# A differential attention stage with a new order of work on every engine

## The chip, the cores and the metric

The kernel runs on one core of a Trainium2 chip. A core has five engines that run their own instruction lists and meet only at semaphores: PE (TensorE, matmuls into the eight PSUM banks), DVE (VectorE), ACT (ScalarE), POOL (GpSimd) and SP (SyncE, which here only issues DMAs). The metric is the device time of one execution in microseconds (us).

## The reference

Two post-norm residual layers over 512 positions of width 1024, in float32. Layer 0 mixes tokens by a chunked spatial gate, layer 1 by differential attention; behind each mixer comes a gated feed-forward block with a width-3 convolution. The change lies in the attention alone:

```python
q, k, v = split(x @ w_qkv)            # 8 heads; q and k as 2 halves of 64, v 128 wide
logits  = q_half @ k_half.T / 8 + bias[head]
probs   = softmax(logits)             # 2 maps of 512 x 512 per head
attn    = probs[0] - lam * probs[1]
o       = attn @ v                    # 512 x 128 per head
o       = o * rsqrt(mean(o * o) + eps) * subln_g * (1 - lambda_init)
y       = concat(o) @ w_out
```

## The kernel before, in words

**Numbers in two halves.** Every float32 operand of a large product is split in a high half (a copy rounded to the PE's fast 32-bit format, made by ACT) and a low half (the difference, made by DVE). `product` then issues three matmuls: high by high, high by low, low by high. Weights come in units of 128 x 2048 elements (1 MB): SP loads a unit into `w_raw`, ACT casts it to `w_hi` (`weights`, L336 and L556), DVE subtracts to get `w_lo` (L602). All three are double-buffered; a unit's cast waits until PE has finished with the unit two before it (`w_used`), a unit's load until the low half of the unit two before it is made (`w_lo_done`), and PE waits for the low half (`unit_ready`).

**The attention stage of before, in order.** First the values of all heads: `tokens_first` (units `U_BV` and the next, heads 0 to 3) and `tokens_group` (two more units, heads 4 to 7), each 96 matmuls with 512 columns, copied by ACT to `v_tok` as plain float32. Then for heads 0 and 1 the query and key projections (`project`, one unit a head, 48 matmuls: 8 blocks of 3 for the queries into bank 0, 8 for the keys into bank 1), and the four score tiles of head 0. Then a loop over heads, `head(h)`, in which PE transposes the mixed probabilities of head h (`turn_probs`, 4 steps of 4 transposes), computes the score tiles of head h+1 (`scores`, 4 tiles of 6 matmuls into banks 2 and 3), multiplies probabilities by values (`values`, 4 steps of 3 matmuls into bank 7), projects head h+2, and does one plain float32 matmul for the mean of squares (`mean_square`, L1308).

**What the other engines do for a head.** ACT: `probs_hi` (4 casts, L534), `exps` (8 exponentials, L525, each with a read of its sum), the cast of the next weight unit (L556), `squares` (L541), `v_head` (high half of the head's values, L515), `query_key` (L508) and `root` (logarithm, L547, and exponential, L551, each behind a table load). DVE: `probs_lo` (L931), `scored` (8 additions of the bias with a row minimum, L901), `mixed` (reciprocal L909, scaling L911, factor L913, mixing L917), the low half of the next weight unit (L602), `v_head` (L888), `query_key` (L877, L880) and `values` (L939). POOL issues the bias loads (L1471, L1477); its only arithmetic in the stage is the tiny `rstd` of the normalisation (L1465).

**The order is written out by hand**: each engine works its list in program order, so an instruction that waits holds up all behind it on its engine. In `head`, ACT does all `exps(h+1)`, then the weight cast, and only then `squares(h)`; PE comes to `mean_square(h)` after the first 24 matmuls of the projection.

**The tail.** Head 7's probabilities are turned around the first half of out-projection unit 0 (`out_unit`, 48 matmuls a unit, four token tiles, two column halves); the rest of units 0 and 1 follows, then `outward` does units 2 and 3.

## Time and profile before

| | us |
|---|---|
| median of 3 runs | 1385.53 |
| lowest and highest of them | 1384.03, 1385.91 |
| span of the profiled execution | 1384.8 |
| PE busy in it | 1310.7 |
| DVE busy | 676.2 |
| ACT busy | 460.4 |
| POOL busy | 64.5 |
| mean granted PE clock | 0.979 of full speed |

The page gives the profiled execution by its span, from the first to the last instruction; its own time beside the span is not listed. A busy PE is not the same as a PE at its peak, because matmuls overlap: a 128x512 matmul shows 0.39 us but the next starts 0.23 us after it. So times of PE work are read from start to start. L numbers are lines of the kernel before.

### The profile page before, as it was taken

To read this page: it belongs to the slowest core of one execution; us is meant where nothing else is said; L and a number is where in the kernel's file an instruction comes from. 1 tells how busy PE (TensorE), PEld (TensorE's weight loads), DVE (VectorE), ACT (ScalarE), POOL (GpSimd) and SP (SyncE) were. 2 spreads that over 40 slices of the span, in tenths; PEclk is the share of its full clock that TensorE was granted. 3 is DMA by queue.
4 is the path that set the end of the run, shared out by engine and by line. 5 is a ranking of instruction groups with operands and counts; after the bars stand their busy time and mean duration, and the time that the engine had idled before them with its cause. 6 is when DMAs were issued, how large, how long until landed. Compare 5 with 4: busy or idle time off the path is not lost.

```text
span 1384.8 us, 15759 instructions
## 1 busy us (share of the span) xinstructions
PE 1310.7 (95%) x6046; PEld 1070.9 (77%) x6046; DVE 676.2 (49%) x875; ACT 460.4 (33%) x549; POOL 64.5 (5%) x82
## 2 busy tenths in 40 slices
PE   7999999998999999999989889897999999999996
PEld 5788887888888888888868566665788888888884
DVE  2537664347433443323652677775664333443227
ACT  2422232213323232223222476765233223232220
POOL 3002000001000000000010100000010000000001
PEclk9999998999999999999999899998999999999998
DMA  7236931231322223223233232221222322223221
GB/s 287 91 92 143 237 107 61 91 122 62 120 92 91 91 91 111 102 91 121 87 98 95 79 99 76 81 87 61 73 80 92 119 93 91 91 91 110 103 91 61
DMA packets 96487, 140.54 MB, mean 101 GB/s; under 512 B 5120, under 2 KB 74840, under 8 KB 96192
## 3 DMA queue, kind: packets, MB, share of 16 engines
q1 hardware_dynamic: 88608, 119.55, 26.5%
q0 software_dynamic: 7840, 20.46, 5.3%
q8 instruction: 26, 0.43, 0.1%
q14 instruction: 13, 0.11, 0.0%
HBM read 137.85 MB, written 10.52 MB: 107 GB/s over the span
## 4 chain that ended last, share of the span: by engine, by line
PE 79%; DVE 10%; ACT 3%; DMA 3%; issue 3%; POOL 1%; DVEq 0%; POOLq 0%; SPq 0%; ACTq 0%
PE bank L990 27%; PE bank L994 25%; PE bank L993 25%; DMA w_raw<-in_a_w_in_dram 3%; DVE w_lo L602 2%; DVE x_tok L626 1%; ACT w_hi L336 1%; DVE r_stat L630 1%; POOL r_rs L1465 1%; DVE x_tok L646 1%; DVE prob L901 1%; PE bank L1308 1%; DVE xt_lo L608 1%; PE bank L1283 1%; DVE s_lo L616 1%
## 5 line engine op out<-in xcount | busy, mean ns | idle before, releaser
L990 PE MATMUL bank<-xt_hi,w_hi 128*128 128x512 f32 (+1 forms) x1024 | 391.2, 382 | 8.1 <-DVE xt_lo L608 6.6
L994 PE MATMUL bank<-xt_hi,w_lo 128*128 128x512 f32 (+1 forms) x1024 | 386.3, 377 | 0.0
L993 PE MATMUL bank<-xt_lo,w_hi 128*128 128x512 f32 (+1 forms) x1024 | 386.3, 377 | 0.0
L602 DVE TENSOR_TENSOR w_lo<-w_raw,w_hi 128x2048 fp32r<-128x2048 f32 x106 | 242.6, 2289 | 292.4 <-ACT w_hi L336 266.1
L990 PEld LDWEIGHTS bank<-xt_hi,w_hi 128*128 128x128 f32 x1024 | 194.1, 190 | 49.7 <-issue 10.3
L336 ACT CAST w_hi<-w_raw 128x2048 fp32r<-128x2048 f32 x60 | 114.5, 1909 | 323.9 <-PE bank L990 271.6
L993 PEld LDWEIGHTS bank<-xt_lo,w_hi 128*128 128x128 f32 x1024 | 194.1, 190 | 35.7 <-issue 1.4
L994 PEld LDWEIGHTS bank<-xt_hi,w_lo 128*128 128x128 f32 x1024 | 194.0, 189 | 35.4
L990 PE MATMUL bank<-w_hi,s_hi 128*128 128x512 f32 x544 | 214.9, 395 | 5.4 <-DVE s_lo L616 5.4
L993 PE MATMUL bank<-w_lo,s_hi 128*128 128x512 f32 x544 | 213.1, 392 | 0.0
L994 PE MATMUL bank<-w_hi,s_lo 128*128 128x512 f32 x544 | 212.9, 391 | 0.0
L990 PEld LDWEIGHTS bank<-w_hi,s_hi 128*128 128x128 f32 x544 | 103.1, 189 | 28.9 <-issue 7.8
L476 ACT CAST w_hi<-w_raw 128x2048 fp32r<-128x2048 f32 x42 | 80.0, 1906 | 134.3 <-PE bank L990 134.3
L993 PEld LDWEIGHTS bank<-w_lo,s_hi 128*128 128x128 f32 x544 | 103.2, 190 | 21.4 <-issue 0.2
L994 PEld LDWEIGHTS bank<-w_hi,s_lo 128*128 128x128 f32 x544 | 103.0, 189 | 21.6
L836 DVE SCALAR_TENSOR_TENSOR conv<-bank,conv_p,conv 128x511 f32<-128x511 f32 x44 | 33.0, 750 | 149.8 <-ACT conv L463 149.8
L463 ACT ACTIVATE conv<-bank,conv_p 128x512 f32<-128x512 f32 x44 | 34.3, 780 | 178.5 <-PE bank L994 178.5
L990 PE MATMUL bank<-w_hi,xt_hi 128*128 128x512 f32 x192 | 77.9, 406 | 13.3 <-DVE w_lo L602 10.9
L853 DVE TENSOR_TENSOR act<-conv,bank 128x512 f32 (+1 forms) x44 | 30.2, 687 | 98.8 <-PE bank L994 98.8
L994 PE MATMUL bank<-w_hi,xt_lo 128*128 128x512 f32 x192 | 76.5, 399 | 0.0
L993 PE MATMUL bank<-w_lo,xt_hi 128*128 128x512 f32 x192 | 76.5, 399 | 0.0
L1465 POOL TENSOR_TENSOR r_rs<-r_ve,neg_half 128x1 f32<-128x1 f32 x16 | 27.3, 1706 | 1011.4 <-DVE r_ve L634 1011.4
(132 smaller groups left out, 1134.4 us busy)
## 6 DMA issues: line engine op xcount, KB each, us to landing
w_raw<-in_f_w_in_dram SPq DMA_DIRECT2D x44, 1024.0 KB, 5.1
w_raw<-in_f_w_down_dram SPq DMA_DIRECT2D x22, 1024.0 KB, 4.8
w_raw<-in_a_w_in_dram SPq DMA_DIRECT2D x16, 1024.0 KB, 5.6
bias_by_query_key<-bias_by_distance POOLq DMA_DIRECT2D x4, 2048.0 KB, 35.9
w_raw<-in_a_w_out_dram SPq DMA_DIRECT2D x8, 1024.0 KB, 4.9
bias_sb<-bias_by_query_key POOLq DMA_DIRECT2D x32, 256.0 KB, 2.9
w_raw<-in_b_w_qkv_dram SPq DMA_DIRECT2D x16, 512.0 KB, 4.9
w_raw<-in_b_w_qkv_dram SPq DMA_DIRECT2D x4, 1024.0 KB, 5.1
```

The lines of the kernel that those rows point to most:

```text
L336: act_e.copy(w_hi[:, u % 2, :], w_raw[:, u % 2, :]).then_inc(w_hi_done, 1)
L463: act_e.activation(conv[:, j, :], bank[j][:, :], ACT.Identity, bias=conv_col(l, NCP - 1, off + j), scale=conv_col(l, 1, off + j)).then_inc ...
L476: act_e.copy(w_hi[:, u % 2, :], w_raw[:, u % 2, :]).then_inc(w_hi_done, 1)
L602: dve.tensor_tensor(w_lo[:, u % 2, :], w_raw[:, u % 2, :], w_hi[:, u % 2, :], ALU.subtract).then_inc(w_lo_done, 1)
L608: ins = dve.tensor_tensor(xt_lo[:, 4 * h:4 * h + 4, t * P:t * P + P], bank[2 * t + h][:, :].rearrange("p (k n) -> p k n", n=P), xt_hi[:, 4 ...
L616: dve.tensor_tensor(s_lo[:, k % 2, :, :], src[:, bass.ds(i * (2 * step) + 2 * k, 2), :] if step else src[:, 2 * k:2 * k + 2, :], s_hi[:, k ...
L836: dve.scalar_tensor_tensor(out=conv[:, j, 1:S], in0=bank[j][:, 0:S - 1], scalar=conv_p[:, l, bass.ds(off + j, 1)], in1=conv[:, j, 1:S], op ...
L853: dve.tensor_tensor(dst, conv[:, j, :], bank[2 + j][:, :], ALU.mult).then_inc(act_done, 1)
L990: ins = pe.matmul(o, a_hi, b_hi, start=start, stop=False)
L993: pe.matmul(o, a_hi, b_lo, start=False, stop=False)
L994: return pe.matmul(o, a_lo, b_hi, start=False, stop=stop)
L1465: pool.tensor_tensor(r_rs[:, t:t + 1], r_ve[:, t:t + 1], neg_half[:, 0:1], ALU.pow).then_inc(rstd_done, 1)
```

## The change

**Units.** The two units of values for heads 4 to 7 are cut the other way: `U_V45` and `U_V67` hold all 1024 rows for two heads each, so that their products have 256 columns (`value_pair`: 24 matmuls a token tile, 96 a unit). The order of units is now: values 0 to 3 (two units), queries and keys of head 0, V45, queries and keys of heads 1 to 7, V67, the out projection.

**Values** are split into `val_hi` and `val_lo` straight from PSUM when they are made (`values_hi`, `values_lo`), for all heads; `v_head` goes away on both engines.

**PE.** Score tiles of head 0 stand between the four tiles of `value_pair(U_V45)`; in the loop the projection of head h+2 is cut into pieces that stand between the transposes and score tiles; `value_pair(U_V67)` stands between the score tiles of head 7; the out projection begins after head 6's values and goes on in pieces through head 7.

**ACT and DVE.** The lists are interleaved tile by tile: the weight cast stands between the second and third `probs_hi`, `squares(h)` before the last two `exps`; `root` loads its first table before it waits. `mixed` is cut in `weighed` and `mixed`.

**POOL** makes the low halves of the 13 units from `U_QK0` to `U_BO + 2`, each as four 128x512 subtractions, and issues no bias loads any more. **SP** issues those between the weight loads. The bias tiles now lie where the normalisation's gains lie, so that they are loaded after the second normalisation, and the third one's gains after the last score.

**Loops** over heads with registers become plain unrolled lists. Unit 2 of the out projection is held in the memory of `val_hi` and `val_lo` of heads 0 to 3.

The core of the diff:

```diff
-    U_QK = U_BV + D * KD // UC
-    U_BO = U_QK + 2 * D * KD // UC
+    U_QK0 = U_BV + 2
+    U_V45 = U_BV + 3
+    U_QK1 = U_BV + 4
+    U_V67 = U_QK1 + H - 1
+    U_BO = U_V67 + 1
...
+        def hi_of(u):
+            if u == U_BO + 2:
+                return val_hi[:, 0:H // 2, :, :].rearrange("p h t n -> p (h t n)")
+            return w_hi[:, u % 2, :]
...
+                if n == 2:
+                    sp.wait_ge(sc_done, 2 * TB * H)
...
+            load_qk(0)
+            load_unit(U_V45, cols(b_w_qkv[0], 2 * D + NB, 2 * P), dst=raw(U_V45, 2 * P))
+            sp.wait_ge(bias_made, 1)
+            sp.wait_ge(rows_ready, TB * 2)
+            load_bias(0)
+            load_qk(1)
+            load_qk(2)
+            for h in range(1, H - 2):
+                load_bias(h)
+                load_qk(h + 2)
+            load_bias(H - 2)
+            load_unit(U_V67, cols(b_w_qkv[0], 2 * D + NB + 2 * P, 2 * P), dst=raw(U_V67, 2 * P))
+            load_bias(H - 1)
...
+                if u == U_BO + 2:
+                    act_e.wait_ge(pv_mm, H // 2)
+                elif u >= 2:
                     act_e.wait_ge(w_used, u - 1 + more(step))
-                act_e.copy(w_hi[:, u % 2, :], w_raw[:, u % 2, :]).then_inc(w_hi_done, 1)
+                act_e.copy(hi_of(u), w_raw[:, u % 2, :]).then_inc(w_hi_done, 1)
...
+            def root(h):
+
+                act_e.preload_act_table_set("natural_log")
+                act_e.wait_ge(ms_mm, h + 1)
...
+            weights(U_QK0)
+            for n in range(TB):
+                values_hi(n)
+            weights(U_V45)
+            query_key(0, 0)
+            query_key(0, 1)
+            weights(U_QK1)
+            exps(0, 0)
+            values_hi(TB)
+            exps(0, 1)
+            exps(0, 2)
+            values_hi(TB + 1)
+            exps(0, 3)
+            weights(U_QK1 + 1)
+            query_key(1, 0)
+            query_key(1, 1)
+            for h in range(H - 2):
+                probs_hi(h, 0)
+                probs_hi(h, 1)
+                weights(U_QK1 + h + 2)
+                probs_hi(h, 2)
+                probs_hi(h, 3)
+                exps(h + 1, 0)
+                exps(h + 1, 1)
+                query_key(h + 2, 0)
+                exps(h + 1, 2)
+                squares(h)
+                exps(h + 1, 3)
+                root(h)
+                query_key(h + 2, 1)
+            h = H - 2
+            probs_hi(h, 0)
+            probs_hi(h, 1)
+            weights(U_BO)
+            probs_hi(h, 2)
+            probs_hi(h, 3)
+            exps(h + 1, 0)
+            values_hi(TB + 2)
+            exps(h + 1, 1)
             stationary(o_t, None, 0, o_done, 2)
+            exps(h + 1, 2)
+            values_hi(TB + 3)
+            exps(h + 1, 3)
             weights(U_BO + 1)
+            squares(h)
             stationary(o_t, None, 1, o_done, 4)
-            head(H - 1)
-            outward(o_t, U_BO, U_F[1] - U_BO, o_done, H, begun=True)
+            root(h)
+            h = H - 1
...
+            h = H - 1
+            probs_hi(h, 0)
+            probs_hi(h, 1)
+            probs_hi(h, 2)
+            probs_hi(h, 3)
+            weights(U_BO + 2)
+            squares(h)
+            root(h)
+            stationary(o_t, U_BO + 1, 2, o_done, 6)
+            weights(U_BO + 3)
+            stationary(o_t, U_BO + 2, 3, o_done, H)
+            weights(U_F[1])
...
+            def weighed(h, t):
+
                 n = TB * h + t
-                dve.wait_ge(exp_done, 2 * n + 2 + (0 if i is None else i * (4 * TB)))
+                dve.wait_ge(exp_done, 2 * n + 2)
                 dve.reciprocal(rsum[:, t, :], psums[:, t, :]).then_inc(rs_done, 1)
-                dve.wait_ge(rs_done, n + 1 + dyn4)
+                dve.wait_ge(rs_done, n + 1)
+                dve.tensor_scalar(c1[:, t:t + 1], rsum[:, t, 1:2], neg_lam[:, 0:1], None, ALU.mult
+                                  ).then_inc(c1_done, 1)
...
+            for n in range(TB):
+                values_lo(n)
+            query_key(0, 0)
+            query_key(0, 1)
+            scored(0, 0)
+            weighed(0, 0)
+            values_lo(TB)
+            scored(0, 1)
+            mixed(0, 0)
+            weighed(0, 1)
+            scored(0, 2)
+            mixed(0, 1)
+            weighed(0, 2)
+            values_lo(TB + 1)
+            scored(0, 3)
+            mixed(0, 2)
+            weighed(0, 3)
+            mixed(0, 3)
+            query_key(1, 0)
...
+            for h in range(H - 2):
+                query_key(h + 1, 1)
+                probs_lo(h, 0)
+                probs_lo(h, 1)
+                scored(h + 1, 0)
+                probs_lo(h, 2)
+                probs_lo(h, 3)
+                weighed(h + 1, 0)
+                scored(h + 1, 1)
+                mixed(h + 1, 0)
+                weighed(h + 1, 1)
+                query_key(h + 2, 0)
+                scored(h + 1, 2)
+                mixed(h + 1, 1)
+                weighed(h + 1, 2)
+                scored(h + 1, 3)
+                mixed(h + 1, 2)
+                weighed(h + 1, 3)
+                mixed(h + 1, 3)
+                values(h)
...
+                lo = w_lo[:, u % 2, :].rearrange("p (k n) -> p k n", n=2 * P)
+                for k in range(KD):
+                    ins = product(bank[b + t // 2][:, t % 2 * 2 * P:t % 2 * 2 * P + 2 * P], xt_hi[:, k, t * P:t * P + P],
+                                  xt_lo[:, k, t * P:t * P + P], hi[:, k, :], lo[:, k, :], k == 0, k == KD - 1,
+                                  frees if k == 0 else 0)
+                if t % 2:
+                    ins.then_inc(bv_mm, 1)
...
+            project(0, 0, range(KD), 1)
+            project(0, 1, range(KD))
+            for t in range(TB):
+                value_pair(U_V45, 4, t, 1 if t == 0 else 0)
+                scores(0, t)
+            project(1, 0, range(KD), 1)
+            project(1, 1, range(KD))
+            for h in range(H - 2):
+                turn_probs(h, 0, 1)
+                turn_probs(h, 1)
+                project(h + 2, 0, range(0, 2))
+                turn_probs(h, 2)
+                scores(h + 1, 0)
+                turn_probs(h, 3)
+                project(h + 2, 0, range(2, 5))
+                scores(h + 1, 1)
+                values(h, 0)
+                project(h + 2, 0, range(5, KD))
+                scores(h + 1, 2)
+                values(h, 1)
+                values(h, 2)
+                scores(h + 1, 3)
+                values(h, 3)
+                project(h + 2, 1, range(0, 3))
+                mean_square(h)
+                project(h + 2, 1, range(3, KD))
+            h = H - 2
+            turn_probs(h, 0, 1)
+            turn_probs(h, 1)
+            value_pair(U_V67, 0, 0)
+            turn_probs(h, 2)
+            scores(h + 1, 0)
+            turn_probs(h, 3)
+            value_pair(U_V67, 0, 1)
+            scores(h + 1, 1)
+            value_pair(U_V67, 0, 2)
+            scores(h + 1, 2)
+            value_pair(U_V67, 0, 3)
+            scores(h + 1, 3)
+            for k in range(TB):
+                values(h, k)
             out_ready(U_BO, S_BO, 0)
-            out_unit(U_BO, 0, (0, 1), start=True)
-            turn_probs(H - 1, (2, 3))
-            values(H - 1, range(TB))
-            mean_square(H - 1)
-
+            pe.wait_ge(bv_lo_done, TB + 4)
+            out_unit(U_BO, 0, (0,), start=True, frees=1)
+            mean_square(h)
+            h = H - 1
+            turn_probs(h, 0)
+            turn_probs(h, 1)
+            pe.wait_ge(sc_done, 2 * TB * H)
+            out_unit(U_BO, 0, (1,), start=True)
+            turn_probs(h, 2)
+            turn_probs(h, 3)
+            values(h, 0)
+            values(h, 1)
             out_ready(U_BO, S_BO, 1)
-            out_unit(U_BO, 1, (0, 1))
+            out_unit(U_BO, 1, (0,))
+            values(h, 2)
+            values(h, 3)
+            out_unit(U_BO, 1, (1,))
+            mean_square(h)
+            pe.wait_ge(at_lo_done, TB * H)
+            out_unit(U_BO, 0, (2,), start=True, halves=(1,))
+            out_unit(U_BO, 0, (3,), start=True, halves=(0,))
+            out_unit(U_BO, 1, (2,), halves=(1,))
+            out_unit(U_BO, 1, (3,), halves=(0,))
+            pe.wait_ge(ln_done, H)
+            out_unit(U_BO, 0, (2,), start=True, halves=(0,))
             pe.wait_ge(o_done, H)
-            out_unit(U_BO, 0, (2, 3), start=True)
-            out_unit(U_BO, 1, (2, 3), frees=1)
+            out_unit(U_BO, 0, (3,), start=True, halves=(1,))
+            out_unit(U_BO, 1, (2,), frees=1, halves=(0,))
+            out_unit(U_BO, 1, (3,), halves=(1,))
...
+            def weights(u):
+
+                pool.wait_ge(w_hi_done, u + 1)
+                pool.wait_ge(w_lo_done, u)
+                for c in range(4):
+                    part = slice(c * NB, c * NB + NB)
+                    ins = pool.tensor_tensor(lo_of(u)[:, part], w_raw[:, u % 2, part], hi_of(u)[:, part], ALU.subtract)
+                ins.then_inc(w_lo_done, 1)
+            for u in range(U_QK0, U_BO + 3):
+                weights(u)
```

## Rows read from the trace of the kernel before

**Rows 1.** The page: busy time of each engine, and PE's granted clock by slice.
```profile
PE 1310.7 (95%) x6046; PEld 1070.9 (77%) x6046; DVE 676.2 (49%) x875; ACT 460.4 (33%) x549; POOL 64.5 (5%) x82
...
PEclk9999998999999999999999899998999999999998
```

**Rows 2.** Windows by stage: length, busy PE, PEld, DVE, ACT, POOL; PE clock; DMA.
```profile
718.65:743.50 24.85, 22.03 (x98) 17.98 (x97) 6.49 (x3) 7.63 (x9) 0.00 (x0) 1.00 0.46 128
743.50:765.50 22.00, 22.00 (x98) 17.94 (x98) 6.66 (x5) 5.50 (x5) 0.00 (x0) 1.00 0.35 96
765.50:804.90 39.40, 31.60 (x128) 21.48 (x128) 29.74 (x74) 24.09 (x47) 4.38 (x8) 0.83 0.27 77
829.25:853.70 24.45, 21.95 (x104) 15.74 (x103) 18.14 (x41) 15.90 (x29) 2.19 (x4) 1.00 0.31 86
926.50:978.20 51.70, 42.18 (x182) 31.42 (x180) 26.55 (x49) 26.66 (x41) 0.00 (x0) 0.90 0.12 41
...
1003.75:1012.45 8.70, 8.70 (x73) 8.70 (x73) 8.60 (x12) 1.91 (x1) 2.52 (x1) 1.00 0.54 175
```

**Rows 3.** Waits of PE, heads 1 to 5 (804.9 to 926.5).
```profile
PE bank L1308 <- ACT o_sq L541: 8.9, 5, 1.8
```

**Rows 4.** Timeline of PE in head 1: start, length, instruction.
```profile
807.53 1.09 PE L1283 MATMUL bank<-ident,prob 128*128 128x128 f32 x8
808.38 0.47 PE L990 MATMUL bank<-at_hi,vh_hi 128*128 128x512 f32 x1
...
817.10 0.50 PE L990 MATMUL bank<-qk_hi 64*128 64x512 f32 x2
...
818.01 0.50 PE L990 MATMUL bank<-xt_hi,w_hi 128*128 128x512 f32 x1
...
822.80 1.12 PE L1308 MATMUL bank<-o_sq,ones 128*128 128x512 f32 x2 [1.78 <-ACT o_sq L541]
```

**Rows 5.** Timeline of PE around two waits for the low half of a unit.
```profile
695.86 0.79 PE L990 MATMUL bank<-w_hi,xt_hi 128*128 128x512 f32 x1 [3.04 <-DVE w_lo L602]
696.45 0.63 PE L993 MATMUL bank<-w_lo,xt_hi 128*128 128x512 f32 x1
...
699.35 0.40 PE L994 MATMUL bank<-w_hi,xt_lo 128*128 128x512 f32 x1
...
718.26 0.39 PE L994 MATMUL bank<-w_hi,xt_lo 128*128 128x512 f32 x1
720.70 0.47 PE L990 MATMUL bank<-w_hi,xt_hi 128*128 128x512 f32 x1 [2.05 <-DVE w_lo L602]
```

**Rows 6.** Groups by line in head 1, DVE and ACT: busy us, mean ns.
```profile
L901 DVE CUSTOM_DVE_ANT_0 prob<-bank,bias_sb 128x512 f32<-128x512 f32 x8 | 5.2, 686 | 1.1 <-PE bank L994 1.1
L917 DVE SCALAR_TENSOR_TENSOR prob<-prob,c 128x512 f32<-128x512 f32 x4 | 3.0, 750 | 0.4
...
L602 DVE TENSOR_TENSOR w_lo<-w_raw,w_hi 128x2048 fp32r<-128x2048 f32 x1 | 2.3, 2285 | 0.0
L911 DVE TENSOR_SCALAR prob<-prob,rsum 128x512 f32<-128x512 f32 x4 | 1.9, 487 | 0.1
...
L525 ACT ACTIVATE prob<-prob,nmax 128x512 f32<-128x512 f32 x8 | 5.7, 717 | 5.1 <-DVE nmax L901 5.1
...
L556 ACT CAST w_hi<-w_raw 128x2048 fp32r<-128x2048 f32 x1 | 1.9, 1889 | 0.0
...
L547 ACT ACT_TABLE_LOAD x1 | 1.3, 1283 | 0.0
```

**Rows 7.** Groups by line of POOL over the whole span.
```profile
L1465 POOL TENSOR_TENSOR r_rs<-r_ve,neg_half 128x1 f32<-128x1 f32 x16 | 27.3, 1706 | 1011.4 <-DVE r_ve L634 1011.4
...
L1437 POOL TENSOR_TENSOR v_rs<-v_ve,neg_half 128x4 f32<-128x4 f32 x1 | 1.1, 1052 | 96.8 <-DVE v_ve L747 96.8
...
L1410 POOL IOTA dist_row<- 32x1024 f32 x1 | 1.0, 974 | 0.0
```

**Rows 8.** DMA issues: count, KB each, median us to landing.
```profile
w_raw<-in_b_w_qkv_dram SPq DMA_DIRECT2D x16, 512.0 KB, 4.9
```

More of the change, by code:

```diff
@@ L322, in landed_count @@
             same = [v for v in range(u % 2, u + 1, 2)]
-            return 16 * sum(2 if U_QK <= v < U_BO else 1 for v in same)
+            return 16 * sum(2 if v == U_QK0 or U_QK1 <= v < U_V67 else 1 for v in same)
         @block.scalar
@@ L581, in _, with exps @@
-            with act_e.Fori(0, H // 2 - 2) as i:
-                for j in range(2):
-                    head(j, i, lambda: qk_weights(U_QK + j + 3, i))
-            head(H - 4, None, lambda: weights(U_QK + H - 1))
-            head(H - 3, None, lambda: weights(U_BO))
-            head(H - 2)
+            def exps(h, t):
+                for j in range(2):
+                    act_e.wait_ge(sc_done, 2 * TB * h + 2 * t + j + 1)
+                    act_e.activation(prob[:, t, j, :], prob[:, t, j, :], ACT.Exp, bias=nmax[:, t, j:j + 1],
+                                     scale=-1.0, accum_out=psums[:, t, j:j + 1]).then_inc(exp_done, 1)
@@ new lines, in probs_hi, with squares @@
+            def probs_hi(h, k):
+                act_e.wait_ge(at_mm, TB * h + k + 1)
+                if k == 0 and h >= 1:
+                    act_e.wait_ge(pv_mm, h)
+                act_e.copy(at_hi[:, k, :], bank[5 + k % 2][:, :]).then_inc(at_hi_done, 1)
+            def squares(h):
+                act_e.wait_ge(pv_mm, h + 1)
+                if h >= 1:
+                    act_e.wait_ge(ms_mm, h)
+                act_e.activation(o_sq[:, :], bank[7][:, :], ACT.Square).then_inc(sq_done, 1)
@@ L963, in _, with probs_lo @@
[L963 to L973 removed]
+            def probs_lo(h, k):
+                dve.wait_ge(at_hi_done, TB * h + k + 1)
+                dve.tensor_tensor(at_lo[:, k, :], bank[5 + k % 2][:, :], at_hi[:, k, :], ALU.subtract
+                                  ).then_inc(at_lo_done, 1)
@@ L974, in _ @@
+            scored(h + 1, 3)
+            mixed(h + 1, 2)
+            weighed(h + 1, 3)
+            mixed(h + 1, 3)
+            stationary(o_t, S_BO + 1, 1)
+            values(h)
+            h = H - 1
+            for k in range(TB):
+                probs_lo(h, k)
+            values(h)
+            stationary(o_t, S_BO + 2, 2)
+            weights(U_BO + 3)
+            stationary(o_t, S_BO + 3, 3)
             enter(3, U_F[1])
@@ new lines, in turn_probs @@
+            def turn_probs(h, k, frees=0):
+                n = TB * h + k
+                if n >= 2:
+                    pe.wait_ge(at_lo_done, n - 1)
+                else:
+                    pe.wait_ge(bv_lo_done, TB + 2)
+                for t in range(TB):
+                    if k == 0:
+                        pe.wait_ge(mixp_done, TB * h + t + 1)
+                    ins = pe.transpose(bank[5 + k % 2][:, t * P:t * P + P], prob[:, t, 0, k * P:k * P + P],
+                                       ident[:, :])
+                    if k == t == 0 and frees:
+                        ins.then_inc(w_used, frees)
+                ins.then_inc(at_mm, 1)
@@ new lines, in _ @@
+            h = H - 2
+            turn_probs(h, 0, 1)
[10 more added lines that the diff above has]
+            scores(h + 1, 3)
+            for k in range(TB):
+                values(h, k)
+            out_ready(U_BO, S_BO, 0)
```

397 lines of the change are left out of this document (138 added, 259 removed).

## The prediction

> **What bounds the kernel now.** I read the page first, then windows by stage, then the waits of PE, then its timeline for one head. PE is busy 95% of the span, no other engine more than half of it, and its granted clock is full except in a few slices, two of them in the middle [rows 1]. So time is gained only by issuing PE work more densely. The windows show where that is possible [rows 2]. From the end of `tokens_first` (718.65) to the start of out-projection unit 2 (978.2) the stage takes 24.85 + 22.0 + 39.4 + 121.6 + 51.7 = 259.5 us; the 121.6 are five heads (804.9 to 926.5) of which one stands there with 24.45. The projection window is solid work: 96 matmuls in 22.0 us, 0.227 us each, 1.00 clock. The window of head 0 is not (PE busy 31.6 of 39.4, clock 0.83), nor is the tail (42.2 of 51.7, clock 0.90), and a middle head has 2.5 us of idle PE. In the heads the wait that ends last is the one for the squares, 8.9 us in five heads [rows 3]: 1.78 us each time, because ACT reaches `squares` only behind eight exponentials and a weight cast [rows 4].
>
> **The price of PE's work.** Eight transposes take 0.85 us (807.53 to 808.38), a score tile 0.91 (817.10 to 818.01) [rows 4]; its two products use different halves of the array rows and overlap. The matmul behind a tile is drawn out (0.50 instead of 0.39), so I take 1.12 with the switch back. A head of PE work, none of it changed by the edit, is then: projection 48 x 0.227 = 10.9; values 12 x 0.227 = 2.7; four score tiles 4.5; sixteen transposes 1.7, with switches 1.9; mean square 1.0. Sum 21.0, against 24.4 now. The 3.4 between them are the 1.78 for the squares, 0.6 at the first score tile, and small waits for DVE in the tiles.
>
> **Step 1, do the waits go away in the loop?** I lay out one head from its first transpose with the lengths of [rows 6]. ACT casts two probability tiles by 1.7, the weight unit by 3.6, the other two by 4.9. PE turns, projects two blocks, turns, scores tile 0 from 2.7, tile 1 near 6.1, tile 2 near 10, tile 3 near 12.5, and values end near 14. Eight row minima at 0.65, four scaling and mixing groups at 1.6 follow on DVE, which mixes the last tile by about 17.6; PE wants that at 21. `squares` now stands ahead of the last two exponentials and ends near 14.7; PE wants it near 16. The logarithm starts at 17.3, its second table load and the exponential end at 20; DVE's `values` comes at 20.7. So PE bounds the head. DVE loses the low half of the unit (2.29) and of the head's values (0.69): 18.14 to 15.2 busy. ACT loses 0.6: 15.9 to 15.3. Both lie beside 21 us of PE. For three more switches of operand shape I add 0.3: **21.3 a head**, 3.1 less than now. Weight units: the load is issued behind the last bias load, near 15.5, and the cast wants it at 1.7 + 21.3 = 23; landing takes 4.9 [rows 8], so some 2.5 us are spare, at an issue gap that the trace doesn't show but that can't be below nothing.
>
> **Step 2, the low halves on POOL.** No row has POOL subtracting 512 columns. From below: not faster than DVE, 2.29 a unit [rows 6]. From above: four instructions with the 1.71 of its tiny 128x1 one, plus three streams of 2048 elements at the 0.95 ns of the iota (974 ns for 1024) [rows 7] = 6.8 + 5.8 = 12.6. Near 128x4, 1.05 us, four make 4.2; with part of the streams beside it I take **5.0**, and keep 2.3 and 12.6 for the range. The Trainium skill (GPSIMD Engine Reference, Elementwise side-by-side cycle accounting) gives 4.5 us for 2048 elements in one instruction on this engine; by that the sum would be half a us less. In the loop, 5.0 lies between the cast's end at 3.6 and the next head's first projection at 22: hidden, and hidden at 12.6 too. It is exposed once. Now PE stops at 718.65 and waits 2.05 us for a low half that DVE makes from 718.26 [rows 5]. POOL would be ready at 723.3: PE stands 4.7 us. After a wait of 3.04 the eight matmuls from 695.86 up to 699.35 took 3.5 us instead of 1.8, at lengths of 0.63 for 0.39, the pace of the lower clock level, where 2.05 cost none [rows 5]; I charge 1.7 for that. So 6.4 us from 718.65 to full pace.
>
> **Step 3, head 0.** Projections of heads 0 and 1: 96 matmuls, 21.8. `value_pair(U_V45)`: 96 matmuls of 256 columns; 72 such took 8.70 us in the feed-forward entry [rows 2], 0.121 each, so 11.6. Four score tiles 4.5. Between two score tiles PE has 2.9 us, DVE 2.9 of minimum, scaling and mixing, and what is left over hides in the 10.9 of head 1's projection, behind which the last mixed tile is wanted. With 0.5 for switches: **38.4**. V45's own low half is wanted 10.9 after its cast may start and takes 1.9 + 5.0: hidden; from a unit of 9 on it is not.
>
> **Step 4, the loop.** Six heads (0 to 5) at 21.3: **127.8**.
>
> **Step 5, heads 6 and 7 and out units 0 and 1.** Transposes of two heads 3.8, V67 11.6, score tiles 4.5, values 5.4, 96 out matmuls 21.8, two mean squares 2.0: 49.1. One wait I can't remove: ACT runs `root(6)` before `probs_hi(7, 0)`, and root has two table loads of 1.28 and waits for the mean square; the first cast of head 7 comes some 1.9 us later than PE wants to turn the third tile. **51.0**. The wait for the first s_lo (3.5 us) and the slow clock that follows it now (window clock 0.90) are gone, because the out work lies beside ready work.
>
> **Sum.** 6.4 + 38.4 + 127.8 + 51.0 = 223.6 against 259.5: 35.9 us less. Bias loads on SP in place of POOL: 32 issues that wait for scores, each followed only by loads with spare time (step 1): nothing; if the cover were gone, each late us delays a cast and then two probability casts, which have about 1 us of slack. The third normalisation's gains are loaded after the last score, some 40 us before use: nothing. `rstd` waits behind POOL's 13 units: the last, U_BO + 2, is made 10 us or more before the normalisation: nothing. All else is as before. The sum is made against the span of 1384.8; the median is 1385.53, 0.7 more. 1385.5 - 35.9 = **1349.6**.
>
> **The rivals.**
> *A. POOL and DVE get in each other's way.* Scaling (L911) and mixing (L917) read two tiles, or one at double pace, from SBUF: 487 and 750 ns for 512 columns [rows 6]. POOL works from 3.6 to 8.6 of the head, where DVE has the first scaling and mixing. If such a pair excludes each other, DVE can lose up to four times one POOL instruction, 5 us a head; the mixed tile then comes at 22.6, the root at 25, with the queries' cast behind it: about 2 us a head on PE's path, 12 in all: 1361.5. For it: `weights` on POOL falls in every head. Against it: DVE's row minima and probability halves read one operand from PSUM, and one or two meetings cost 1.2, which the slack takes. The Trainium skill (SBUF — State Buffer, Who interferes with whom) says just this: a DVE instruction with two SBUF inputs and a GpSimd one exclude each other for a whole instruction; no row here can show it, since POOL does no large arithmetic. Chance 0.17.
> *B. A unit takes POOL 9 to 12.6 us.* Start +4 to +7.6, V45 up to +3.6, head 2's unit (cast behind head 0's last exponentials, wanted 11.8 into the stretch) +3 to +6.7, out unit 1 up to +3: 10 to 21 more, middle 1365. Chance 0.09.
> *C. The change does not do what it says:* the loop stays at 24.4 because each removed wait comes back at another tile, as with DVE's minima before the next score tile, which wait for PE and PE for them. Then only steps 3 and 5 gain, 35.9 - 6 x 3.1 = 17.3: 1368. For it: DVE sits between every pair of score tiles. Against it: PE has 2 us of projection between them. Chance 0.07.
> *D. Slower.* POOL becomes the bound of the stage. Twelve units in a row up to out unit 1 take 12 U from 718.2, and some 15 us of PE follow; that passes 978 from U = 20 on, that is 5.1 us for one subtraction of 512 columns; at U = 22, 1409. Beyond the upper bound of step 2, but that bound is from other operations. Chance 0.04.
>
> **How the numbers follow.** The forecast, with 0.63, has its own range of 1343 (unit at 2.3, no switches, head 7 without its wait) to 1357 (a head of 22.5). The rest is A, B, C and D. The range to report takes in A and the nearer part of B: 1343 to 1365; left out are C, D and the far end of B, and a little below. No case lies near no change. 0.2% (2.8 us) is about what a measurement of this kernel can tell from no change. All but D are faster: 0.95; D 0.04; 0.01 between.
>
> **What would show it.** In the trace after: a gap of about 4.7 us in PE near 718, followed by slow matmuls, ended by POOL; POOL subtractions of about 1.25 us in fours; head periods of 21.3 with no wait for o_sq; PE's clock 1.00 through the loop; out unit 2 starting near 942. Step 1 is wrong if a head takes over 22.5 us, and then the wait at its transposes or scores names the engine. A is shown by scaling or mixing instructions of over 1 us beside POOL's, B by POOL's mean, D by PE waiting for POOL in every head. Most likely to make the number wrong: small waits at many points of the loop, for each 0.5 us a head is 3 us.

## The result and the profile after

The changed kernel takes 1346.58 us (median of four, 1345.44 to 1347.60) against 1385.36 for the kernel before (median of four): the ratio is 0.9724, 95% interval 0.9710 to 0.9738. Forecast was 1349.6. The profiled execution has a span of 1345.6 us against 1384.8. Of the runs below one, of the kernel with head 0's score tiles behind V45, took 1639.11 us at a mean granted clock of 0.748, and is left out of its median and ratio.

Windows of the kernel after, with the columns of [rows 2]: PE's stop at the start of the stage, the stretch from there to head 0's first transpose, one head of the loop (head 1), the whole loop of six heads, and heads 6 and 7 up to out-projection unit 2.

```profile
717.65:722.25 4.60, 0.00 (x0) 0.02 (x1) 2.48 (x4) 1.43 (x3) 4.51 (x4) 0.97 0.01 2
722.25:761.50 39.25, 39.24 (x216) 32.85 (x217) 15.10 (x37) 15.83 (x25) 15.11 (x12) 0.96 0.38 108
782.50:803.50 21.00, 21.00 (x104) 15.20 (x103) 15.37 (x40) 15.55 (x28) 5.24 (x4) 1.00 0.37 102
761.50:887.55 126.05, 126.05 (x613) 91.28 (x612) 91.16 (x234) 93.04 (x168) 31.39 (x24) 1.00 0.35 101
887.55:939.25 51.70, 49.46 (x277) 40.03 (x276) 24.21 (x49) 29.46 (x43) 16.03 (x12) 1.00 0.29 101
```

The first number is the length, the second PE's busy time. In the loop they are equal: the profile shows no idle time of PE in 126 us. Its granted clock there is 1.00, as it was in the loop before [rows 2]; in head 0's stretch it is 0.96, where the window of head 0 before had 0.83, and in heads 6 and 7 it is 1.00, where the tail had 0.90. The stage, from the end of `tokens_first` to out unit 2, has shrunk from 259.5 us to 4.6 + 39.25 + 126.05 + 51.7 = 221.6. That is 37.9 of the span's 39.2; the other 1.3 lie outside it (the stage begins 1.0 earlier).

All waits of PE in the stage after (from 717 to 940; us in total, times, longest):

```profile
PE bank L1065 <- POOL w_lo L1594: 4.6, 1, 4.6
PE bank L1369 <- DVE at_lo L971: 1.5, 1, 1.5
PE bank L1065 <- DVE qk_lo L936: 0.6, 1, 0.6
```

The wait for the squares [rows 3] is gone. Timeline of ACT and then of PE in head 1 of the kernel after, to compare with [rows 4]: the squares are ready at 797.9, the mean square starts at 799.17 without a wait, straight behind the ninth matmul of the key projection.

```profile
797.29 0.60 ACT L566 ACTIVATE o_sq<-bank 128x512 f32<-128x512 f32 x1 [1.03 <-PE bank L1069]
797.78 0.71 ACT L553 ACTIVATE prob<-prob,nmax 128x512 f32<-128x512 f32 x1
```

```profile
798.94 0.39 PE L1069 MATMUL bank<-xt_hi,w_lo 128*128 128x512 f32 x1
799.17 1.02 PE L1393 MATMUL bank<-o_sq,ones 128*128 128x512 f32 x2
```

The start of the stage, to compare with [rows 5]: POOL makes the unit's low half in four subtractions of together 4.95 us, PE stands 4.63 us, and the next seven matmuls (722.26 to 725.38) run at 0.43 from start to start, at lengths of 0.63: the lower clock level.

```profile
717.21 4.95 POOL L1594 TENSOR_TENSOR w_lo<-w_raw,w_hi 128x512 fp32r<-128x512 f32 x4 [15.39 <-ACT w_hi L372]
```

```profile
722.26 0.76 PE L1065 MATMUL bank<-xt_hi,w_hi 128*128 128x512 f32 x1 [4.63 <-POOL w_lo L1594]
722.82 0.63 PE L1068 MATMUL bank<-xt_lo,w_hi 128*128 128x512 f32 x1
723.25 0.63 PE L1069 MATMUL bank<-xt_hi,w_lo 128*128 128x512 f32 x1
```

### The profile page after: what moved, and what is told of

It reads as the page before. It is cut to its first block, busy times and chain, and to the rows that moved or that the text cites. A ratio compares the mean times of both kernels' runs of the same rounds, so it can differ in the third digit from the quotient of the medians.

```text
span 1345.6 us, 15635 instructions
## 1 busy us (share of the span) xinstructions
PE 1298.6 (97%) x6142; PEld 1068.4 (79%) x6142; DVE 648.7 (48%) x862; ACT 456.7 (34%) x541; POOL 115.0 (9%) x103
## 4 chain that ended last, share of the span: by engine, by line
PE 88%; DVE 7%; POOL 2%; ACT 1%; issue 1%; DMA 0%; POOLq 0%; DVEq 0%; ACTq 0%
PE bank L1065 29%; PE bank L1069 28%; PE bank L1068 28%; DVE w_lo L649 2%; DVE x_tok L673 1%; DVE r_stat L677 1%; POOL r_rs L1582 1%; DVE x_tok L693 1%; PE bank L1369 1%; DVE xt_lo L655 1%; ACT w_hi L372 1%; PE bank L1079 1%; PE bank L1393 0%; POOL w_lo L1594 0%; DVE s_lo L663 0%
## 5 line engine op out<-in xcount | busy, mean ns | idle before, releaser
L649 DVE TENSOR_TENSOR w_lo<-w_raw,w_hi 128x2048 fp32r<-128x2048 f32 x93 | 212.8, 2289 | 246.5 <-ACT w_hi L372 220.2
L372 ACT CAST w_hi<-w_raw 128x2048 fp32r<-128x2048 f32 x63 | 120.4, 1911 | 299.4 <-PE bank L1065 255.1
L1065 PE MATMUL bank<-w_hi,s_hi 128*128 128x512 f32 x528 | 207.8, 394 | 1.5 <-DVE s_lo L663 1.5
L1069 PE MATMUL bank<-w_hi,s_lo 128*128 128x512 f32 x528 | 206.3, 391 | 0.0
L1068 PE MATMUL bank<-w_lo,s_hi 128*128 128x512 f32 x528 | 206.2, 390 | 0.0
L512 ACT CAST w_hi<-w_raw 128x2048 fp32r<-128x2048 f32 x42 | 80.1, 1907 | 134.4 <-PE bank L1065 134.4
L1065 PEld LDWEIGHTS bank<-w_hi,s_hi 128*128 128x128 f32 x528 | 99.7, 189 | 23.7 <-issue 3.3
L1069 PEld LDWEIGHTS bank<-w_hi,s_lo 128*128 128x128 f32 x528 | 99.5, 188 | 20.9
L1068 PEld LDWEIGHTS bank<-w_lo,s_hi 128*128 128x128 f32 x528 | 99.7, 189 | 20.6 <-issue 0.2
L1065 PE MATMUL bank<-w_hi,xt_hi 128*128 128x512 f32 (+1 forms) x224 | 84.4, 377 | 11.5 <-DVE w_lo L649 8.3
L1069 PE MATMUL bank<-w_hi,xt_lo 128*128 128x512 f32 (+1 forms) x224 | 82.4, 368 | 0.0
L1068 PE MATMUL bank<-w_lo,xt_hi 128*128 128x512 f32 (+1 forms) x224 | 82.4, 368 | 0.0
```

Of the source, the lines that this page charges most:

```text
L372: act_e.copy(hi_of(u), w_raw[:, u % 2, :]).then_inc(w_hi_done, 1)
L512: act_e.copy(w_hi[:, u % 2, :], w_raw[:, u % 2, :]).then_inc(w_hi_done, 1)
L649: dve.tensor_tensor(w_lo[:, u % 2, :], w_raw[:, u % 2, :], w_hi[:, u % 2, :], ALU.subtract).then_inc(w_lo_done, 1)
L1065: ins = pe.matmul(o, a_hi, b_hi, start=start, stop=False)
L1068: pe.matmul(o, a_hi, b_lo, start=False, stop=False)
L1069: return pe.matmul(o, a_lo, b_hi, start=False, stop=stop)
```

## The experiments

The forecast was close, so the open question was not how much but which part. The first group takes parts of the change away or adds one alone; the second looks at POOL. Not run by themselves were: the new cut of the value units, the value halves made straight from PSUM, the bias loads on SP, the unrolled loops, the first table load of `root`, and the place of out unit 2. Times are medians; ratios are to the kernel before on the same chip. For comparison: the changed kernel has 0.9724 (0.9710 to 0.9738), and 0.9721 (0.9708 to 0.9735) when run once more (below).

### ACT's order undone in the loop

```diff
@@ ACT, for h in range(H - 2)
                 probs_hi(h, 1)
-                weights(U_QK1 + h + 2)
                 probs_hi(h, 2)
...
                 exps(h + 1, 2)
-                squares(h)
                 exps(h + 1, 3)
+                weights(U_QK1 + h + 2)
+                squares(h)
                 root(h)
```

> The changed kernel with one thing undone in the loop of six heads: ACT casts the next weight unit and takes the squares behind all eight exponentials, as before, not between them. Theory (ACT's order was a main part of the gain): the mean square waits some 1.9 us in each of six heads, 11 in all: 1358. Rival: the projection now stands in pieces where PE would wait, so the late squares cost nothing: 1347.

Measured: 1363.29 us, ratio 0.9842 (0.9827 to 0.9857), 16.7 more than the changed kernel. PE's waits from 716 to 960:

```profile
PE bank L1393 <- ACT o_sq L566: 13.9, 6, 2.3
```

Six waits of 2.3 us are 13.9, and the matmuls behind one of them (head 1's) ran at the lower clock; behind the other five they did not. The pieces of projection do not cover the late squares. My expected 1.9 a head was 0.4 short. From mean square to mean square a head takes 23.5 to 23.7 us, and the one with the lower clock 25.1.

### One part alone in the kernel before

```diff
@@ ACT, head(h)
                 if h + 1 < H:
-                    exps(h + 1, i)
+                    exps(h + 1, i, (0, 1, 2))
+                squares(h, i)
+                if h + 1 < H:
+                    exps(h + 1, i, (3,))
                 if next_unit is not None:
                     next_unit()
-                squares(h, i)
```

> The kernel before with one part of the change alone: ACT takes the squares of head h between the third and the fourth pair of exponentials, and casts the next weight unit behind the fourth. If the wait for the squares is the main loss of the old loop, each head gives back its 1.8 us and the rest stays: 24.3 to 22.5 in six heads and up to 3 in head 6, 1385.5 - 13 = 1372. Rival: the removed wait comes back at the next tile or at the first transposes (the new order of PE is what counts): less than 5, 1381 or more.

Measured: 1373.98 us, ratio 0.9916 (0.9901 to 0.9931): 10.9 less than the kernel before on that chip (1384.88), of 13 expected. The mean squares of heads 0 to 5 follow each other at 22.1 to 22.4 us, from 24.2 to 24.45 before. The longest of PE's waits from 716 to 975:

```profile
PE bank L1285 <- DVE prob L919: 6.1, 4, 2.1
PE bank L992 <- DVE s_lo L618: 4.0, 3, 3.2
PE bank L992 <- DVE nmax L903: 3.9, 4, 1.7
PE bank L992 <- DVE qk_lo L882: 3.5, 6, 0.6
```

These lie in head 0, in the tail from head 6 on, and 0.6 at each head's first score tile: places that the rest of the change treats. Not all of them are left over from before: the waits for `prob` at the transposes were 3.2 us in two, and the 2.9 more come in two waits, of 1.61 and 1.25, in front of head 7's. So the rival came true in the tail: head 6 won 2.9 us there, as expected, and head 7 lost it again. The squares moved ahead on ACT are, alone, worth over a quarter of the whole gain.

### PE's order undone in the loop

```diff
@@ ACT and DVE: query_key(h + 2, 0) behind the fourth tile
@@ PE, for h in range(H - 2)
                 turn_probs(h, 0, 1)
                 turn_probs(h, 1)
-                project(h + 2, 0, range(0, 2))
-                turn_probs(h, 2)
                 scores(h + 1, 0)
+                turn_probs(h, 2)
                 turn_probs(h, 3)
...
+                scores(h + 1, 2)
+                project(h + 2, 0, range(0, 4))
+                scores(h + 1, 3)
+                project(h + 2, 0, range(4, KD))
+                mean_square(h)
+                project(h + 2, 1, range(KD))
```

> The changed kernel with PE's order in the loop undone: transposes, score tiles and values as before, the query projection in two lumps around the last score tile, the key projection in one. ACT and DVE keep their new order but for the query halves, which follow the fourth tile. If the projection pieces are needed to cover DVE's and ACT's turn between transposes and score tiles, PE waits at the third transposes, values and second tile again, 1.5 to 2 us a head: 10 more than the changed kernel, 1356.5. Rival: ACT's early squares alone made the gain of the loop: 1347.

Measured: 1359.51 us, ratio 0.9809 (0.9792 to 0.9825), 12.9 more than the changed kernel. A head takes 22.97 us from mean square to mean square (801.70 to 824.67), 2.0 more. The waits of PE that the trace names make only 1.2 of it:

```profile
PE bank L1065 <- DVE at_lo L971: 4.2, 6, 0.7
PE bank L1065 <- DVE qk_lo L936: 3.9, 7, 0.6
```

The rest does not show as idle time: in these 22.97 us PE is busy 21.73, against 20.98 in a head of the changed kernel. Most of it is one score tile, which takes 1.50 us (816.46 to 817.96) instead of 0.91:

```profile
816.46 0.49 PE L1065 MATMUL bank<-qk_hi 64*128 64x512 f32 x1
...
817.07 0.50 PE L1065 MATMUL bank<-qk_hi 64*128 64x512 f32 x1
```

Its two products do not start together as elsewhere but 0.61 us apart, the distance of the two row minima of DVE (815.71 and 816.32) that free their banks. PE is held there, but the first product keeps it busy meanwhile. So both orders are needed: ACT's without PE's leaves 22.3 in the old kernel and 22.97 here, PE's without ACT's 23.5, and together they make 21.0.

### Score tiles of head 0 behind V45

```diff
@@ PE
             for t in range(TB):
                 value_pair(U_V45, 4, t, 1 if t == 0 else 0)
+            for t in range(TB):
                 scores(0, t)
```

> The changed kernel with the four score tiles of head 0 behind the whole of value_pair(U_V45) in place of between its tiles. The tiles then follow each other at DVE's pace, 9.5 us for four in the kernel before against 4.5: 5 more, and 1 or so for a clock that falls in the waits: 1352.5. Rival: the projection of head 1 behind them takes it up: 1347.

Measured: 1355.06 us (median of three), ratio 0.9779 (0.9761 to 0.9797), 8.5 more than the changed kernel instead of 6. PE waits 3.7 us for DVE's minima, and the windows show what the waits bring with them (last three columns: PE clock, DMA share, GB/s):

```profile
745.00:750.00 5.00, 4.12 (x28) 3.07 (x26) 1.31 (x4) 1.42 (x4) 0.00 (x0) 1.00 0.00 0
750.00:756.00 6.00, 3.22 (x10) 2.03 (x11) 5.48 (x17) 2.90 (x10) 0.00 (x0) 0.54 0.32 87
756.00:760.00 4.00, 4.00 (x12) 2.77 (x11) 3.65 (x10) 2.39 (x7) 0.00 (x0) 0.50 0.23 66
```

In the ten us from 750 PE ran at half its clock, four of them without any idle time. The same 24 score matmuls are cheap between value tiles and dear in a row.

### Head 7's order undone

```diff
@@ ACT: squares(H - 2) ahead of weights(U_BO + 1)
@@ PE
-            out_unit(U_BO, 0, (0,), start=True, frees=1)
             mean_square(h)
             h = H - 1
             turn_probs(h, 0)
             turn_probs(h, 1)
-            out_unit(U_BO, 0, (1,), start=True)
+            out_unit(U_BO, 0, (0, 1), start=True, frees=1)
...
-            (values and out unit 1 in turns, column halves apart)
+            values(h, 0) ... values(h, 3); mean_square(h)
+            out_unit(U_BO, 1, (0, 1)); out_unit(U_BO, 0, (2, 3)); out_unit(U_BO, 1, (2, 3))
```

> The changed kernel with PE's order in head 7 undone: mean square of head 6 directly behind its values, out unit 0's first half in one piece between the transposes, head 7's values in one piece, then its mean square, then the rest of out units 0 and 1 in the old order; ACT takes head 6's squares before it casts out unit 1. If the pieces of the out projection cover the squares and probability halves of heads 6 and 7, these waits are back: 0.8 at each mean square, 0.9 more at the third transposes, 0.4 at the values, and 1 to 2 for the clock: 4 more than the changed kernel, 1350.5. Rival: the out work covers them in either order: 1347.

Measured: 1349.74 us, ratio 0.9748 (0.9735 to 0.9762), 3.5 more than the changed kernel run beside it. PE's waits from 880 to 945:

```profile
PE bank L1369 <- DVE at_lo L971: 2.1, 1, 2.1
PE bank L1393 <- ACT o_sq L566: 1.4, 2, 0.7
```

The mean squares wait as expected (0.7 each for 0.8), the transposes 0.6 longer than in the changed kernel (0.9 expected); the 0.4 at the values did not come. That is 2.0 us of the 3.5. The profiled execution took 1354.70 us, 5.0 above the median of its runs, so the rest can't be read from this trace. Of the four parts that were undone this one is worth least.

### The first unit's low half back on DVE

```diff
@@ DVE (ACT likewise: values_hi of three tiles, weights, the fourth)
-            for n in range(TB):
+            for n in range(TB - 1):
                 values_lo(n)
+            weights(U_QK0)
+            values_lo(TB - 1)
@@ POOL
-            for u in range(U_QK0, U_BO + 3):
+            for u in range(U_V45, U_BO + 3):
```

> The changed kernel, but the low half of unit U_QK0 alone is made by DVE again (POOL begins with V45), and ACT and DVE split the first three value tiles before that unit instead of behind it. If POOL's slower subtraction and the slow clock behind the wait are what the start costs, PE's wait of 4.6 us falls to about 2.0 and the matmuls behind it run at full pace: 4.3 us less than the changed kernel, 1342.3. Rival: the clock falls after the shorter wait as well: 2.6 less, 1344.0. Rival: something else was due next there (the value splits): no gain, 1346.6.

Measured: 1341.07 us, ratio 0.9680 (0.9667 to 0.9693), faster than the changed kernel by 5.5 by the medians (on two chips), 3.7 by the spans (1341.9 against 1345.6). Timeline of DVE and of PE at that place:

```profile
717.50 2.29 DVE L650 TENSOR_TENSOR w_lo<-w_raw,w_hi 128x2048 fp32r<-128x2048 f32 x1 [3.57 <-ACT w_hi L372]
```

```profile
719.90 0.47 PE L1068 MATMUL bank<-xt_hi,w_hi 128*128 128x512 f32 x1 [1.94 <-issue]
720.20 0.40 PE L1071 MATMUL bank<-xt_lo,w_hi 128*128 128x512 f32 x1
720.44 0.40 PE L1072 MATMUL bank<-xt_hi,w_lo 128*128 128x512 f32 x1
```

PE stands 1.94 us in place of 4.63 (the trace names no releaser, but DVE's low half ends at 719.79) and the matmuls behind follow at 0.24, the higher clock level: 2.7 of the gain is the wait, 1.6 the clock. So the move of this unit to POOL cost about what the sum had charged for it (4.3). The order of the value splits was changed with it, but in both traces the low half starts as ACT's cast of the unit ends (717.21 and 717.50), so they are not what made PE start earlier. The 1.6 is not certain: the kernel of the last section, when run again, has the same wait of 1.94 with slow matmuls behind it.

### All low halves on DVE

As the run before, and DVE makes the other twelve too. In the loop it does so behind the last mixed tile:

```diff
@@ DVE, for h in range(H - 2)
                 mixed(h + 1, 3)
+                weights(U_QK1 + h + 2)
                 values(h)
@@ POOL
-            for u in range(U_QK0, U_BO + 3):
-                weights(u)
```

> As the first, but the low halves of all 13 units are made by DVE, none by POOL; in the loop DVE makes them behind the last mixed tile, where it stands idle for 2.4 us before the values. If the new order alone removed the waits, DVE has room for this: head period stays at 21.0 and the time is that of the first run, 1342.3 (within 1). Rival: the move to POOL was needed: DVE delays values and the query and key halves by 1 us or more a head, period 22 to 23, 1349 to 1355.

Measured: 1343.78 us, ratio 0.9696 (0.9682 to 0.9710); its interval overlaps that of the run before it and touches that of the changed kernel, its span is 1342.5. The period of a head is 20.94 to 21.00 us, as with POOL. Timeline of DVE in head 1:

```profile
796.59 0.75 DVE L965 SCALAR_TENSOR_TENSOR prob<-prob,c 128x512 f32<-128x512 f32 x1
797.26 2.29 DVE L648 TENSOR_TENSOR w_lo<-w_raw,w_hi 128x2048 fp32r<-128x2048 f32 x1
799.70 0.75 DVE L976 SCALAR_TENSOR_TENSOR o_t<-bank,sub_g,o_rs 128x512 f32<-128x512 f32 x1 [0.15 <-ACT o_rs L576]
```

The 2.29 us fit into the hole in which DVE otherwise waits for `root` (2.36 us in the changed kernel), to within 0.15. The order made the gain; the move of the low halves to POOL was not needed for it. By medians the changed kernel is 2.8 us slower than this one, by ratios 0.28%, or 3.9 us, at intervals that just touch.

### POOL's work doubled

```diff
@@ POOL, weights(u)
+                for c in range(4): (the same four subtractions)
+                ins.then_inc(bias_made, 1); pool.wait_ge(bias_made, u - U_QK0 + 2)
                 for c in range(4):
```

> The changed kernel with each of POOL's subtractions done twice, so that a unit takes about 10 us instead of 5. If POOL's work is hidden in the loop, the head period stays at 21.0 and only the exposed places pay: the first unit 5, V45 about 1.5, head 2's unit 2.8, out unit 1 some 2.8: 12 in all, 1358.6. Rival (POOL and DVE exclude each other for a whole instruction, and this reaches PE): scaling and mixing lengths of over 1 us in most heads, period 22 to 23, 1365 or more.

Measured: 1363.53 us, ratio 0.9845 (0.9825 to 0.9864), 17 more than the changed kernel. PE's waits for POOL make 14.5, of which 4.6 were there before (9.6 at the first unit, 2.7 at head 2's, 1.7 at out unit 1, 0.5 at V45), so 9.9 more, as the first theory had it but smaller at V45 and out unit 1. The remaining 7 or so are rival A with the clock behind it. In each of four heads from 804 on one scaling and one mixing last 1.2 us in place of 0.48 and 0.75; three heads grew by about 0.5. In the head of 872 to 899 the timeline of DVE shows three such instructions:

```profile
884.68 1.60 DVE L957 TENSOR_SCALAR prob<-prob,rsum 128x512 f32<-128x512 f32 x1
886.21 0.68 DVE L946 CUSTOM_DVE_ANT_0 prob<-bank,bias_sb 128x512 f32<-128x512 f32 x1
...
887.42 1.81 DVE L966 SCALAR_TENSOR_TENSOR prob<-prob,c 128x512 f32<-128x512 f32 x1
...
889.48 1.20 DVE L957 TENSOR_SCALAR prob<-prob,rsum 128x512 f32<-128x512 f32 x1
```

The row minimum between them, which reads one operand from PSUM, keeps its 0.68. The timeline of PE in the same head: the last score tile waits for DVE, and the windows (here length, PE busy, PE clock, DMA share, GB/s) show the clock that falls with it.

```profile
891.93 0.50 PE L1065 MATMUL bank<-qk_hi 64*128 64x512 f32 x1 [1.67 <-DVE nmax L946]
```

```profile
885.00:890.00 5.00, 5.00 (x24) 1.00 0.22 76
890.00:895.00 5.00, 3.33 (x10) 0.75 0.18 52
895.00:900.00 5.00, 5.00 (x14) 0.57 0.69 240
```

That head took 26.6 us from mean square to mean square (872.75 to 899.37) instead of 21.0. A wait of 1.67 us thus cost 5.6, in slow matmuls and in a score tile whose products no longer overlap. The result lies between the theory and its rival: the instructions of over 1 us are there in every head from 804 on, but only one period rose by more than 0.7.

### A version that beats both

The kernel with the first unit's low half on DVE, and for head 7:

```diff
@@ ACT
-            root(h)
             h = H - 1
             probs_hi(h, 0)
             probs_hi(h, 1)
+            root(h - 1)
@@ DVE
             mixed(h + 1, 3)
+            weights(U_BO + 1)
             stationary(o_t, S_BO + 1, 1)
-            values(h)
             h = H - 1
-            for k in range(TB):
-                probs_lo(h, k)
+            (probs_lo 0 and 1, values(h - 1), probs_lo 2 and 3)
@@ POOL: without unit U_BO + 1
@@ PE
             turn_probs(h, 3)
-            values(h, 0)
-            values(h, 1)
             out_ready(U_BO, S_BO, 1)
             out_unit(U_BO, 1, (0,))
+            values(h, 0)
+            values(h, 1)
```

> The first run's kernel (U_QK0's low half on DVE) with two more edits for head 7: ACT casts the first two probability tiles before root(6), PE does the first piece of out unit 1 ahead of the values of head 7, and DVE makes the low half of out unit 1, so that POOL does not hold up s_lo. Expected: PE's wait of 1.5 us at the third transposes goes, nothing new comes: 1.5 below the first run, 1339.6. Rival: the wait moves to head 7's values, which now need root(6) later: 1341.

Measured: 1340.60 us, ratio 0.9683 (0.9670 to 0.9697), span 1338.9. PE's waits from 716 to 975 (those for xt_lo and x_tok come behind the stage):

```profile
PE bank L1071 <- DVE xt_lo L656: 3.3, 2, 2.5
PE bank L1071 <- issue: 1.9, 1, 1.9
PE bank L1085 <- DVE x_tok L694: 0.6, 1, 0.6
PE bank L1071 <- DVE qk_lo L937: 0.6, 1, 0.6
PE bank L1071 <- DVE s_lo L664: 0.4, 1, 0.4
```

The wait of 1.5 us at the transposes has gone and none has come in its place. By the times alone it can't be told from the version with the first edit only (0.9680); by the traces head 7's mean square follows head 6's after 13.65 us (905.61 to 919.26), where it took 15.56 with the first edit only (907.80 to 923.36). It was run again beside the changed kernel:

> The kernel with the first unit's low half on DVE and the new order in head 7, once more, on the same chip as the changed one: by PE's waits in its trace (1.9 in place of 4.6 without a slow clock behind it, none of 1.5 at the transposes) 5.8 below the changed kernel: 1340.8. Rival: what was gained in head 7 is lost again, 1342.3.

Measured: 1340.11 us, ratio 0.9686 (0.9673 to 0.9700). PE's wait at the start is 1.94 us again, but now eight matmuls behind it run at the lower clock level:

```profile
718.31 0.73 PE L1071 MATMUL bank<-xt_hi,w_hi 128*128 128x512 f32 x1 [1.94 <-issue]
718.84 0.63 PE L1074 MATMUL bank<-xt_lo,w_hi 128*128 128x512 f32 x1
719.26 0.63 PE L1075 MATMUL bank<-xt_hi,w_lo 128*128 128x512 f32 x1
```

So the reason given for 5.8, a start without a slow clock, did not hold in this execution, though the number did.

> The changed kernel itself once more, beside the other two on the same chip: 1346.6, within 1.5.

Measured: 1346.24 us, ratio 0.9721 (0.9708 to 0.9735). On one chip the new version is 6.1 us faster than the changed kernel, and the intervals are apart. The two traces, both with slow matmuls at the start, account for 4.5 of it: 2.7 in the first wait and 1.8 in head 7.

## Why the prediction was right, step by step

**Where time was to be gained.** Right: it came from denser PE work in the stage, 37.9 us there against 35.9 forecast, with PE's busy time and length equal in the loop.

**Step 1, the loop.** Right in mechanism, 0.3 too long in size: 21.0 us a head, not 21.3. The 21.0 of PE work already held the switches; the 0.3 for three more of them was not needed. Of the 3.4 us to be won, the forecast put down what was neither squares nor first score tile to small waits in the tiles; the idle time of a head before (2.5) has no room for them, but there too a score tile stood with its products 0.61 us apart (835.19 and 835.80), which does not show as idle. The layout on the other engines held: DVE busy 15.4 (15.2 forecast), ACT 15.6 (15.3), squares ready 15.4 us into the head (14.7) and wanted at 16.7. Taking either order back brings the waits back (2.5 and 2.0 us a head).

**Step 2, POOL.** The unit took 4.95 us (5.0 taken, 2.3 and 12.6 the bounds), the wait 4.6 (4.7), with the slow matmuls behind it (about 1.5 us lost, for 1.7). That 5.0 came out is in part luck: it was chosen between bounds of 2.3 and 12.6, near a POOL instruction of 128x4. The Trainium skill's figure for one instruction of 2048 elements (GPSIMD Engine Reference, Elementwise side-by-side cycle accounting), 4.5 us, is for an addition; the four subtractions of 1.24 each take 0.45 more together. In the loop the work was hidden; doubled, it was still hidden from the projections but for head 2's unit.

**Steps 3 and 5.** 39.25 us with the slow matmuls in it, against 38.4 + 1.7; and 51.7 against 51.0. So the errors go both ways: 0.95 too long up to the loop, 1.75 too long in it, 0.7 too short behind it, 2.0 too long in all. The other 1.0 between 1349.6 and 1346.58 lies outside the stage, where the spans differ by 1.3 us and the sum had nothing; what changed there is open. The wait that I placed behind `root(6)` is there, with 1.5 us for the 1.9 forecast; one of 0.63 for the key half at head 6 I had left out: there PE goes from the transposes straight to V67, whose banks need it.

**Rivals.** A was right as a mechanism and wrong as a price: POOL and DVE do hold each other up, but in the changed kernel each of POOL's units in the loop grows only from 5.0 to 5.24 us, and scaling from 0.48 to 0.57. In head 0 one scaling lasts 1.31 us, which costs PE nothing there. The largest meeting is in head 7, where POOL's unit takes 5.97 and the low half of 1024 columns 2.21 in place of 1.22:

```profile
911.23 5.97 POOL L1594 TENSOR_TENSOR w_lo<-w_raw,w_hi 128x512 fp32r<-128x512 f32 x4 [14.98 <-ACT w_hi L372]
```

```profile
912.61 2.21 DVE L663 TENSOR_TENSOR s_lo<-o_t,s_hi 128x1024 fp32r<-128x1024 f32 x1 [2.26 <-ACT s_hi L395]
```

With PE's order undone, one scaling in each head lasts 1.27 us, and the row minimum behind it still starts 0.13 us after the matmuls that it waits for, as where no scaling is held up. Only in the kernel with POOL's work doubled does a wait of PE follow from such a meeting. The Trainium skill (SBUF — State Buffer, Who interferes with whom) says that a DVE instruction with two SBUF inputs contends with a GpSimd one that reads SBUF, that `tensor_scalar` can do so in a 2-port mode, and that one with at most one SBUF input outside these modes does not. The traces agree: mixing and the low half have two SBUF inputs, scaling is a `tensor_scalar`, and the row minima, with one operand in PSUM, keep their 0.68. B's mechanism was tested by the doubled kernel: a unit of 10 us costs 10 us in exposed waits, the near end of what was forecast for 9 to 12.6. C did not come: the period fell to 21.0. D was not approached; by its own terms (12 x 22 + 15 from 718.2) its 1409 should have been 1404 or 1405.

**What the forecast did not say:** that the move to POOL is a net loss of some 3 to 4 us (2.8 by medians, 3.9 by ratios) inside a gain of 39. It charged 4.3 for it at the start (2.6 for the wait, 1.7 for the clock) and set nothing against that in the loop, and so had the answer without drawing it.

## What to carry to other kernels

When one engine bounds a stage, lay its work out by start-to-start times and ask of every other engine's list where its next result is due; the squares moved ahead on ACT gave 11 us of 39 by themselves. Undone one at a time, ACT's order in the loop costs 16.7 us, PE's there 12.9, the interleaving in head 0 8.5 and head 7's order 3.5. That is 41.6 in all, about the 38.8 won and the 3 to 4 lost on POOL; but parts that lean on each other are counted twice in such a sum, so it does not show that nothing else helped. Before giving work to a second engine, look for a hole in the first one's list: DVE had 2.4 us free at the right place for a 2.3 us job, and the slower engine only added a wait where there was no cover. Price a wait with the clock behind it.

## What the runs showed of the hardware

- **A wait of PE can cost more than its length.** After 4.6 us, 7 to 11 matmuls ran at 0.43 us in place of 0.23, in each of the six traces that have this wait (in one of them only from the fourth matmul on). After 2.3 us that happened once in six times, and after 1.94 us in one trace of four. 1.67 us in the doubled kernel, between values and a score tile, was followed by several us at clocks of 0.75 and 0.57, and cost 5.6 in all; and three waits of together 3.7 brought ten us at 0.54 and 0.50. What decides between these cases the runs don't settle; the length of the wait alone does not, since the same wait in the same place went both ways.
- **POOL and DVE hold each other up, both ways:** with one scaling in its way a unit of POOL takes 5.24 for 5.04 us, with a 1024-column subtraction 5.97; scaling takes up to 1.60 for 0.48 and mixing up to 1.81 for 0.75, the latter two in the doubled kernel. A row minimum, with one operand in PSUM, keeps its 0.68 beside POOL's work.
- **Four 128x512 float32 subtractions take POOL 4.95 us,** DVE 2.29 us for the same 2048 columns in one.
- **Score tiles with 64 rows overlap:** six matmuls of 512 columns in 0.90 us, where six with 128 rows take 1.36. Where the second product has to wait for its bank, the tile takes up to 1.50, and none of it shows as idle time.
